# Two transformer blocks on one core: 1024 instead of 512 bytes a partition for the descriptors of GpSimd's DMAs, and a table of constants without one unread block

## The chip, the cores and the metric

One core of one Trainium2 chip runs the kernel. A time is that of one execution on the device in microseconds (us), and a kernel's time is the median over its runs. Before the change it is 4043.69 us, from two runs of 4041.86 and 4045.51 us.

## The reference

Two model blocks run one after the other over 512 tokens of width 1024, each with two layers, all in fp32. The parts that take most of the time are the SwiGLU stages and the other projections. There are six SwiGLU stages: two in each layer of the first block (width 2816) and one in each layer of the second (`FFN_HIDDEN`, the same).

```python
def swiglu(h, w_gate, w_up, w_down):
    return (jax.nn.silu(h @ w_gate) * (h @ w_up)) @ w_down

def first_block(...):
    for l in range(DEPTH):
        x = x + 0.5 * swiglu(rms_norm(x, ffn1_norm[l]), ffn1_w_gate[l], ffn1_w_up[l], ffn1_w_down[l])
        h = rms_norm(x, mix_norm[l])
        ...
        x = x + jnp.concatenate([y_a, y_b, y_c], axis=-1) @ w_out[l]
        x = x + memory_cross_attention(rms_norm(x, xa_norm[l]), rms_norm(mem, mem_norm[l]),
                                       xa_wq[l], xa_wkv[l], xa_wo[l])
        x = x + 0.5 * swiglu(rms_norm(x, ffn2_norm[l]), ffn2_w_gate[l], ffn2_w_up[l], ffn2_w_down[l])
    return rms_norm(x, final_norm)

def second_block(...):
    for l in range(DEPTH):
        ...
        h = h + mix @ w_out[l]
        u = rmsnorm(h, ffn_norm[l])
        h = h + (jax.nn.silu(u @ w_gate[l]) * (u @ w_up[l])) @ w_down[l]
    return rmsnorm(h, final_norm)
```

The conv, sparse attention, cross attention, retention and differential attention between them are left out here; the change does not touch them.

## The kernel before

Activations stay in SBUF, transposed, with 128 features on the partitions. Every weight comes in chunks of 128 output columns by 1024 inputs (512 KB, 4 KB a partition). A product is made in three matmuls of rounded fp32 parts: high weight by high input, high by low, low by high. So each chunk has to be split into `w_hi` and `w_lo`. There are four slots (`RING = 4`) for the raw chunk, for `w_hi` and for `w_lo`; chunk n uses slot n % 4.

A chunk passes through these steps, each ordered by semaphores alone:

- SP loads it from HBM into `raw` (`load`, L457), when the low part of the chunk that had the slot before is finished (`wait_split`).
- ACT rounds it into `w_hi` (L1102), when PE has finished the chunk that had the slot before (`tiles`).
- The low part is made in one of two ways. In the mixing and attention stages DVE subtracts (L1562). For the chunks of the list `LOW`, 68 from the fifth chunk of each SwiGLU stage on, ACT writes a second, negated rounding into `w_lo` (L1104), and GpSimd (POOL) issues a DMA from `raw` to `w_lo` that adds in flight (`low`, L2272). The DMA's completion counts up `low_in` of its slot.
- PE waits for the low part (`wait_split`) and multiplies: 8 x 3 matmuls of 128 x 512 (L563, L564, L565).

```python
def low(c):
    pool.wait_ge(rounded, c + RING + 1)
    nc.gpsimd.dma_start(w_lo[:, c % RING, :], raw[:, c % RING, :], accum_op=ALU.add).then_inc(low_in[c % RING], 16)
```

The argument c is that of the chunk before in the slot: `low(c)` finishes chunk c + 4. POOL's code has no wait on `low_in`. 404 chunks go this way.

A SwiGLU stage has 68 chunks in three groups: 8, 8 and 6 tiles of the width, each as turns of four chunks (gate, up, gate, up), 11 turns in all, and 8 down chunks behind each group (six instead of eight blocks deep in the last). In nearly all turns the last two chunks are a fast pair: `fast_pair` makes the 256-column halves with seven products of half size instead of eight (84 matmuls of 128 x 256, L604, L605, L606), for which it needs sums of the weights' quarters. POOL makes these sums from `raw` (`first_sums`, L2288 and L2289, which wait for the loads of both chunks, and `second_sums`, L2294 and L2295); ACT rounds them (`sum_hi`, L1148), DVE makes the rest. In a turn POOL's order is written out by hand:

```python
low(c)
if ahead: first_sums(*pairs[0])
low(c + 1)
if ahead: second_sums(*pairs.pop(0))
low(c + 2)
low(c + 3)
```

Between the down chunks of a stage's last group POOL also squares x for the next norm (L2245, L2246), and DVE adds a finished down chunk to x (L1652).

Constants come in one table, `constants()`, loaded at the start by two DMAs on SP: columns 0 to 255 first (identity and ones), the rest later. Columns are named by `C_ID` and its companions (L60); `C_ROT` is written into the table and read by nothing.
Of the kernel before, what the change touches and what calls it, by code (L numbers as in the profile page):

```python
# [32 lines left out]
P = 128  # L33
# [23 lines left out]
ROUND = 1.5 * 2 ** 23  # L57

C_ID, C_ONE, C_ROT, C_DIST, C_NEG, C_DEC, C_BIG, C_INV = 0, 128, 256, 384, 896, 1408, 1920, 2048  # L60
C_N = C_INV + 1

# [90 lines left out]
def constants():  # L154
    c = np.zeros((P, C_N), np.float32)
    p = np.arange(P)[:, None]
    m = np.arange(S)[None, :]
    c[:, C_ID:C_ID + P] = np.eye(P)
    for j in range(P):
        c[j + 32 if j % 64 < 32 else j - 32, C_ROT + j] = 1.0  # L160
    dist = 384 + p - m
    c[:, C_DIST:C_DIST + S] = dist
    c[:, C_NEG:C_NEG + S] = np.where(dist >= 0, 0.0, -BIG)
    c[:, C_DEC:C_DEC + S] = np.where(m - p >= 0, m - p, 1e9)
    c[:, C_BIG:C_BIG + P] = np.where(np.arange(P)[None, :] <= p, 0.0, BIG)
    inv = (10000.0 ** (-np.arange(0, 64, 2) / 64)).astype(np.float32)
    c[:, C_INV] = inv[np.arange(P) % 32] * np.where(np.arange(P) % 64 < 32, 1.0, -1.0)
    c[:, C_ONE:C_ONE + P] = 1.0
    return c
# [2282 lines left out]
```

## Time and profile before

| what | value |
|---|---|
| median of 2 runs | 4043.69 us |
| profiled execution, its own time | 4040.94 us |
| its span, first to last instruction | 4039.1 us |
| PE busy, share of the span | 89% |
| granted clock of PE, mean | 0.965 |
| POOL busy, share of the span | 30% |
| low DMAs (`w_lo<-raw`) | 404 of 512 KB |
| raw loads | 602 |

The profile is of one execution. PE is TensorE's matmuls, DVE VectorE, ACT ScalarE, POOL GpSimd and SP SyncE, whose queue issues the loads. A line number such as L2272 is that of the kernel before. Waits are put down to whatever released the engine last; "issue" stands where the profile shows no releaser. [...]

### The profile page before, as it was taken

To read this page: it belongs to the slowest core of one execution; us is meant where nothing else is said; L and a number is where in the kernel's file an instruction comes from. 1 tells how busy PE (TensorE), PEld (TensorE's weight loads), DVE (VectorE), ACT (ScalarE), POOL (GpSimd) and SP (SyncE) were. 2 spreads that over 40 slices of the span, in tenths; PEclk is the share of its full clock that TensorE was granted. 3 is DMA by queue.
4 is the path that set the end of the run, shared out by engine and by line. 5 is a ranking of instruction groups with operands and counts; after the bars stand their busy time and mean duration, and the time that the engine had idled before them with its cause. 6 is when DMAs were issued, how large, how long until landed. Compare 5 with 4: busy or idle time off the path is not lost.

```text
span 4039.1 us, 50532 instructions
## 1 busy us (share of the span) xinstructions
PE 3596.7 (89%) x18454; PEld 2928.2 (72%) x18454; DVE 1912.6 (47%) x2971; ACT 1791.8 (44%) x2567; POOL 1229.0 (30%) x1035
## 2 busy tenths in 40 slices
PE   8888899998888888879999988889988888998887
PEld 6677686877767677757687776777877667886766
DVE  4333497564324524349756532445644244572423
ACT  5444356345434444435634543434544343453433
POOL 1223375132223422236513232330423131042323
PEclk9999899999999999999999999999999999999999
DMA  7676641426766666664242666642366663246665
GB/s 179 159 163 157 146 110 58 122 79 148 162 156 153 159 157 158 155 150 108 61 118 82 149 157 156 152 119 63 94 156 157 155 154 101 59 113 151 159 150 129
DMA packets 679460, 536.52 MB, mean 133 GB/s; under 512 B 19952, under 2 KB 622984, under 8 KB 679304
## 3 DMA queue, kind: packets, MB, share of 16 engines
q1 hardware_dynamic: 617096, 317.15, 27.7%
q0 software_dynamic: 58176, 211.84, 26.7%
q10 hardware_dynamic: 4032, 5.51, 0.6%
q8 instruction: 91, 1.49, 0.2%
q14 instruction: 65, 0.53, 0.0%
HBM read 314.75 MB, written 2.10 MB: 78 GB/s over the span
## 4 chain that ended last, share of the span: by engine, by line
PE 39%; DMA 24%; issue 18%; POOL 11%; ACT 5%; DVE 3%; ACTq 0%; POOLq 0%; SPq 0%; DVEq 0%
DMA w_lo<-raw 17%; PE bank L563 10%; PE bank L565 10%; PE bank L564 10%; DMA raw<-in_ffn_w_up 2%; ACT w_lo L1104 2%; POOL mem L2246 2%; POOL w_lo L2272 2%; POOL mem L2245 2%; POOL mem L2289 1%; ACT w_hi L1102 1%; PE bank L718 1%; POOL mem L2295 1%; DMA raw<-in_w_up 1%; POOL mem L2294 1%
## 5 line engine op out<-in xcount | busy, mean ns | idle before, releaser
L1102 ACT ACTIVATE w_hi<-raw 128x1024 fp32r<-128x1024 f32 x602 | 635.2, 1058 | 1509.4 <-PE bank L565 1366.6
L563 PE MATMUL bank<-u_hi,w_hi 128*128 128x512 f32 x1920 | 793.8, 413 | 156.6 <-DMA w_lo<-raw 144.0
L2272 POOL DMA_DIRECT2D w_lo<-raw x404 | 356.4, 882 | 1679.3 <-issue 1100.3
L563 PE MATMUL bank<-h_hi,w_hi 128*128 128x512 f32 (+1 forms) x1568 | 636.9, 406 | 174.8 <-DMA w_lo<-raw 162.5
L565 PE MATMUL bank<-u_hi,w_lo 128*128 128x512 f32 x1920 | 779.9, 406 | 0.0
L564 PE MATMUL bank<-u_lo,w_hi 128*128 128x512 f32 x1920 | 777.0, 405 | 0.0
L565 PE MATMUL bank<-h_hi,w_lo 128*128 128x512 f32 (+1 forms) x1568 | 619.9, 395 | 0.0
L564 PE MATMUL bank<-h_lo,w_hi 128*128 128x512 f32 (+1 forms) x1568 | 619.5, 395 | 0.0
L563 PEld LDWEIGHTS bank<-u_hi,w_hi 128*128 128x128 f32 x1920 | 373.7, 195 | 278.2 <-issue 120.7
L563 PEld LDWEIGHTS bank<-h_hi,w_hi 128*128 128x128 f32 x1568 | 303.8, 194 | 290.3 <-issue 156.8
L1652 DVE SCALAR_TENSOR_TENSOR x<-bank,x 128x512 f32 (+1 forms) x192 | 132.6, 690 | 741.4 <-PE bank L565 741.4
L565 PEld LDWEIGHTS bank<-u_hi,w_lo 128*128 128x128 f32 x1920 | 372.6, 194 | 91.4
L564 PEld LDWEIGHTS bank<-u_lo,w_hi 128*128 128x128 f32 x1920 | 374.1, 195 | 86.0
L1104 ACT ACTIVATE w_lo<-raw 128x1024 fp32r<-128x1024 f32 x404 | 421.4, 1043 | 0.0
L565 PEld LDWEIGHTS bank<-h_hi,w_lo 128*128 128x128 f32 x1568 | 303.8, 194 | 69.1
L1562 DVE TENSOR_TENSOR w_lo<-raw,w_hi 128x1024 fp32r<-128x1024 f32 x198 | 280.9, 1425 | 150.7 <-ACT w_hi L1102 150.6
L564 PEld LDWEIGHTS bank<-h_lo,w_hi 128*128 128x128 f32 x1568 | 304.3, 194 | 62.9 <-issue 0.5
L2382 POOL TENSOR_TENSOR mem<-mem,spare 128x512 f32<-128x512 f32 x120 | 171.1, 1464 | 113.2 <-ACT spare L1327 112.9
L604 PE MATMUL bank<-t_hi,sum_hi 128*128 128x256 f32 x684 | 190.0, 278 | 0.0
L605 PE MATMUL bank<-t_lo,sum_hi 128*128 128x256 f32 x684 | 189.6, 277 | 0.0
L606 PE MATMUL bank<-t_hi,sum_lo 128*128 128x256 f32 x684 | 189.4, 277 | 0.0
L1566 DVE SCALAR_TENSOR_TENSOR u_lo<-x,par,u_hi (+1 forms) x88 | 140.8, 1600 | 79.4 <-ACT u_hi L1109 79.4
(302 smaller groups left out, 5969.5 us busy)
## 6 DMA issues: line engine op xcount, KB each, us to landing
w_lo<-raw POOLq DMA_DIRECT2D x404, 512.0 KB, 6.2
raw<-in_w_in SPq DMA_DIRECT2D x96, 512.0 KB, 3.9
raw<-in_ffn_w_gate SPq DMA_DIRECT2D x88, 512.0 KB, 4.0
raw<-in_ffn_w_up SPq DMA_DIRECT2D x88, 512.0 KB, 4.0
raw<-in_ffn_w_down SPq DMA_DIRECT2D x64, 512.0 KB, 4.2
raw<-in_w_gate SPq DMA_DIRECT2D x44, 512.0 KB, 3.9
raw<-in_w_up SPq DMA_DIRECT2D x44, 512.0 KB, 3.9
raw<-in_w_out SPq DMA_DIRECT2D x32, 512.0 KB, 4.1
```

What stands on the lines that cost most here:

```text
L563: mm(o, w_hi[:, s, w], rhs_hi[:, r], start=k == order[0], stop=False)
L564: mm(o, w_hi[:, s, w], rhs_lo[:, r], start=False, stop=False)
L565: ins = mm(o, w_lo[:, s, w], rhs_hi[:, r], start=False, stop=k == order[-1])
L604: mm(o, wh, rh, start=k == 0, stop=False)
L605: mm(o, wh, rl, start=False, stop=False)
L606: ins = mm(o, wl, rh, start=False, stop=k == KT // 2 - 1)
L1102: ins = a(w_hi[:, p.slot, :], raw[:, p.slot, :], ACT.Copy)
L1104: ins = a(w_lo[:, p.slot, :], raw[:, p.slot, :], ACT.Copy, scale=-1.0)
L1562: tt(w_lo[:, p.slot, :], raw[:, p.slot, :], f32(w_hi[:, p.slot, :]), ALU.subtract).then_inc(split, 1)
L1566: stt(dst_lo, src, scale, f32(dst_hi), ALU.mult, ALU.subtract).then_inc(e, 1)
L2272: nc.gpsimd.dma_start(w_lo[:, c % RING, :], raw[:, c % RING, :], accum_op=ALU.add).then_inc(low_in[c % RING], 16)
L2382: tt(conv[n % 2], conv[n % 2], tap_t[n % 4], ALU.add).then_inc(tap_added, 1)
```

## The change

The scratch for the descriptors of POOL's DMAs grows from 512 to 1024 bytes in each partition. The block `C_ROT`, 128 columns of fp32 or 512 bytes in each partition, leaves the table, and the columns behind it move up by 128; `C_N` falls from 2049 to 1921. On SP the DMA of the table's rest moves 1665 columns instead of 1793. No other instruction differs on any engine, and the order on each is as before. The tensors in front of `const` lie 512 bytes further on, those behind it where they were.

```diff
-C_ID, C_ONE, C_ROT, C_DIST, C_NEG, C_DEC, C_BIG, C_INV = 0, 128, 256, 384, 896, 1408, 1920, 2048
+C_ID, C_ONE, C_DIST, C_NEG, C_DEC, C_BIG, C_INV = 0, 128, 256, 768, 1280, 1792, 1920
 C_N = C_INV + 1
...
     c[:, C_ID:C_ID + P] = np.eye(P)
-    for j in range(P):
-        c[j + 32 if j % 64 < 32 else j - 32, C_ROT + j] = 1.0
     dist = 384 + p - m
...
-    nc = bacc.Bacc("TRN2", target_bir_lowering=False, num_devices=1, dynamic_dma_scratch_size=512)
+    nc = bacc.Bacc("TRN2", target_bir_lowering=False, num_devices=1, dynamic_dma_scratch_size=1024)
```

## Rows read from the trace of the kernel before

**Rows 1.** The page: span, busy time of each engine, and the chain that ended last, by engine.

```profile
span 4039.1 us, 50532 instructions
...
PE 3596.7 (89%) x18454; PEld 2928.2 (72%) x18454; DVE 1912.6 (47%) x2971; ACT 1791.8 (44%) x2567; POOL 1229.0 (30%) x1035
...
PE 39%; DMA 24%; issue 18%; POOL 11%; ACT 5%; DVE 3%; ACTq 0%; POOLq 0%; SPq 0%; DVEq 0%
```

**Rows 2.** Stretches: us, PE, PEld, DVE, ACT, POOL busy (count), clock, DMA share, GB/s.

```profile
34.00:480.00 446.00, 381.88 (x1803) 306.42 (x1802) 159.35 (x224) 196.06 (x219) 122.14 (x116) 0.95 0.69 158
...
3610.00:4024.00 414.00, 350.93 (x1846) 290.24 (x1844) 149.75 (x205) 175.17 (x192) 121.13 (x112) 0.97 0.65 149
sum 2575.00, PE 2197.17 PEld 1804.80 DVE 978.38 ACT 1132.46 POOL 762.64; mean PE 366.19 PEld 300.80 DVE 163.06 ACT 188.74 POOL 127.11
...
1800.00:2210.00 410.00, 399.75 (x2053) 316.54 (x2053) 292.26 (x524) 196.56 (x363) 159.86 (x112) 0.99 0.33 92
```

**Rows 3.** Waits: engine, line, waited for: us in total, times, longest.

```profile
POOL w_lo L2272 <- issue: 1100.3, 235, 7.2
...
POOL w_lo L2272 <- ACT w_lo L1104: 559.6, 110, 7.0
...
PE bank L563 <- DMA w_lo<-raw: 306.5, 195, 4.9
...
PE bank L604 <- DMA w_lo<-raw: 20.1, 30, 1.6
```

**Rows 4.** SP in order of time: start us, us, queue, line, op, out<-in.

```profile
1620.94 0.38 SPq L457 DMA_DIRECT2D raw<-in_ffn_w_gate  x1
1627.35 0.38 SPq L457 DMA_DIRECT2D raw<-in_ffn_w_up  x1
1633.87 0.37 SPq L457 DMA_DIRECT2D raw<-in_ffn_w_gate  x1
...
1647.14 0.37 SPq L457 DMA_DIRECT2D raw<-in_ffn_w_gate  x1
```

**Rows 5.** POOL in order of time, same stretch; idle before and its releaser in brackets.

```profile
1621.24 0.86 POOL L2272 DMA_DIRECT2D w_lo<-raw  x1 [6.86 <-ACT w_lo L1104]
1627.64 0.89 POOL L2272 DMA_DIRECT2D w_lo<-raw  x1 [5.54 <-issue]
1634.12 0.87 POOL L2272 DMA_DIRECT2D w_lo<-raw  x1 [5.59 <-issue]
```

**Rows 6.** The tile w_lo: ACT's second rounding, ns min/median/max, and its DMAs' landing.

```profile
L1104 ACT ACTIVATE w_lo<-raw x404: 1038/1043/1055, 33.5 to 4000.9; 128x1024 fp32r<-128x1024 f32 x135
...
DMA to landing us min/median/max: 4.5/6.2/8.0
```

**Rows 7.** DVE in order of time: a chunk of the down projection taken.

```profile
297.21 0.69 DVE L1652 SCALAR_TENSOR_TENSOR x<-bank,x 128x512 f32 x1 [4.91 <-PE bank L565]
```

**Rows 8.** The page: DMA queues, packets, MB, their packets' time as share of the span.

```profile
q1 hardware_dynamic: 617096, 317.15, 27.7%
q0 software_dynamic: 58176, 211.84, 26.7%
```

**Rows 9.** PE in order of time: matmul starts and modelled durations at either clock.

```profile
1623.58 0.63 PE L563 MATMUL bank<-h_hi,w_hi 128*128 128x512 f32 x1
1624.00 0.63 PE L564 MATMUL bank<-h_lo,w_hi 128*128 128x512 f32 x1
...
1624.80 0.40 PE L563 MATMUL bank<-h_hi,w_hi 128*128 128x512 f32 x1
1625.03 0.40 PE L564 MATMUL bank<-h_lo,w_hi 128*128 128x512 f32 x1
```

**Rows 10.** The chain in order of time: a load, the first and the last sum.

```profile
1640.74 3.88 DMA raw<-in_ffn_w_up
...
1644.79 1.28 POOL mem L2288
...
1648.76 1.31 POOL mem L2295
```

## The prediction

> **What bounds the kernel now.** I read the page's first parts, then stretches, then who waits for whom, then two engines side by side around the longest wait. TensorE (PE) is busy 89% of the span, but the chain that ended last gives PE only 39%; 24% of it is DMA and 18% "issue", time in which an engine waited for nothing that the profile shows [rows 1]. So something between DMAs sets part of the time. The stretches say where: in the six SwiGLU stages, together 2575 us of the 4039.1 us span, PE is busy 2197.17 us, 85%, at a granted clock of 0.95 to 0.97; in the stretch 1800:2210, between two such stages, it is busy 399.75 of 410 us at 0.99 [rows 2]. The waits name the late operand: 195 + 30 waits of PE, 306.5 + 20.1 us, end when a DMA `w_lo<-raw` lands. POOL (GpSimd), which issues these DMAs (I call them low DMAs), stood 1100.3 us, 235 times, in front of them for no reason that the profile names [rows 3].
>
> The reason can be read from two engines. SP's load into a raw slot waits, in the code, for the landing of the low DMA that read this slot. SP starts its loads at 1620.94, 1627.35 and 1633.87 [rows 4]. POOL starts its next low DMA at 1621.24, 1627.64 and 1634.12 [rows 5], 0.25 to 0.30 us later each time, although its code waits only for ACT's rounding (to which the first of the three is put down, and 559.6 us in all [rows 3]). So POOL acts as if it too waited for the landing: one low DMA is in flight, never two. From issue to landing one takes 6.2 us at the median [rows 6]; with the gap that is the period of 6.4 to 6.5 us in rows 5. PE needs less: in the down projection DVE takes a finished chunk every 4.91 + 0.69 = 5.60 us where PE does not wait [rows 7]. A serial DMA sets the pace of these stages. 
>
> [...]
>
> **The change part by part: the scratch.** No instruction is added, removed or moved on any engine. The sum is made against the profiled execution's 4040.94 us (span 4039.1), 2.75 us below the median of 4043.69. If a second low DMA fits, POOL issues as soon as ACT has rounded, and three costs go. First, PE's waits that end with a landing, 306.5 + 20.1 = 326.6 us [rows 3]. Second, PE's idle time is counted from the modelled end of a matmul, 0.40 us after its start, while matmuls that don't wait start 0.23 us apart [rows 9]; so each of the 225 waits costs 0.17 us more than is shown, 38 us. Third, the clock: a mean of 0.96 means that 8% of 2575 us, 206 us, ran at 1.2 GHz. There matmuls start 0.42 us apart instead of 0.23 [rows 9], so 45% of the busy part (85%) is lost: 206 x 0.85 x 0.45 = 79 us. I expect it back, since the clock is 0.99 where PE hardly waits [rows 2]. Together 444 us.
>
> A second way gives the same. A turn of four chunks is two plain ones and a fast pair, 48 matmuls of 512 columns and 84 of 256; at 0.233 us (5.60 / 24) and half of it 21.0 us. A down chunk is 5.6 us, or 4.2 in the last group of a stage. Eleven turns, 16 and 8 chunks are 354 us a stage and 2125 for six: 450 below the 2575 of rows 2, which also hold waits of other kinds. So 444 is a ceiling.
>
> **What is late next.** The DMA engines first. The two queues' packets took 26.7% and 27.7% of the span [rows 8], which is 2.67 us for a low DMA (404) and 1.86 us for a load (602): 4.5 us a chunk, under PE's 5.3 to 5.6; in the last groups (six of eight chunks, where loads are three quarters) 4.1 against 4.2. I charge 0.4 us to each of those 48 chunks, 20 us. Next, the slots: a slot is free when PE is done with its chunk and is wanted again three chunks later, after some 16 us. ACT's two roundings of 1.04 us and a landing of 6.2, at most 8.0 [rows 6], are 8.3 to 10.1, so some 6 us are left for queueing. Last, POOL's own order: the sums of weights wait for a load (3.88 us in the chain) and take 1.3 us each, four a turn [rows 10]; the next low DMA is queued behind them on POOL, and ACT's `sum_hi` waits for the last. A landing 6.2, a load 3.9, four sums 5.2 and three low DMAs of 0.9 on POOL make 18 us of a turn of 21; with longer landings it reaches 21. I charge 25 us for this over the stages. That leaves 444 - 45 = 399 us. The ends are nothing and 444.
>
> **The dropped block.** 128 columns are 64 KB less to load at the start, 0.3 us at a low DMA's 512 KB in 2.67 us, beside the other loads there: 0 taken. x, raw, w_hi and w_lo lie 512 bytes further into a partition; no instruction's wait or shape hangs on the address, and nothing in the rows sets one slot apart from another: 0 taken.
>
> The sum: 4040.94 - 399 = 3642, and 3 more for the median: 3645 us.
>
> **The rivals.** *It isn't the scratch.* POOL may take these DMAs one at a time whatever room they have, because they accumulate, or because two don't fit in 1024 bytes either. [...] Against it: nothing in the code orders them, and room is what a DMA on POOL's queue needs besides. The time stays at 4041 to 4044 us. Chance 7%.
>
> *Lifted, but paid to the DMA engines.* Low DMAs and loads now run into each other. The engines are busy 0.65 to 0.69 of these stages [rows 2]; the same work in 2125 us would be 0.67 x 2575 / 2125 = 0.81. If landings stretch so that half of the waits stay, 444 / 2 = 222 us go, about 3820 us. Against it stand the 6 us of room. Chance 12%.
>
> *Slower: loads starved behind low DMAs.* Today a load starts at a landing, ahead of the next low DMA. With several low DMAs queued it would come among their packets. A slot then goes through landing, load, ACT 2.1, low DMA 6.2, and four chunks take 26.2 us today (1620.94 to 1647.14 [rows 4]); when loads take over 26.2 - 8.3 = 17.9 us, against 3.9 now, the kernel becomes slower. If each of a load's 64 packets per engine (617096 packets for some 602 loads on 16 engines) waits for one packet of a low DMA, 2.67 / 8 = 0.33 us, that is 21 + 1.9 us, a turn of 31.2, and over 101 turns 5.0 x 101 = 505 us more: about 4550 us. Against it: the four low DMAs of a turn hold the engines for 10.7 us in all, so a load can hardly wait for 21. Chance 3%. [...]
>
> **How the numbers follow.** My forecast, most of the waits gone, has 78%; its own range is 3560, some 40 us under the ceiling's 3597 since the rows round, to 3780, 260 us gone. The contention case at 3820 lies just above and is still more than 2% faster. The range 3560 to 3780 leaves 2 in 10 outside. Two per cent, 81 us, is about what a measurement of this kernel can tell from no change. Faster by over 2%: 78 + 12 = 90%; within 2%: 7%; slower: 3%.
>
> **What would show it.** Right: "issue" in front of POOL's low DMAs falls from 1100 us to little, and what ends POOL's idle time there is ACT's rounding; low DMAs start less than a landing apart; PE's waits on `w_lo<-raw` fall from 327 to under 60 us; the clock in the six stages rises to 0.98 or more; down chunks come 5.6 us apart throughout; the DMA share there passes 0.75. Landings may grow to 7 or 8 us without harm. Wrong: POOL still starts 0.3 us behind SP at each landing (first rival); or low DMAs overlap, but PE waits for their landing, or ACT and POOL for raw loads, as long as before (second and third).

## The result, and the profile after

The changed kernel takes 3543.71 us (median of two runs, 3534.69 and 3552.73) against 4043.69 before: a ratio of 0.8764, 95% interval 0.8666 to 0.8861. It is 500 us faster, 100 us more than forecast, and lies below the range of 3560 to 3780. The direction and the cause hold; the size was off. Every line number is two less than before, as two lines are gone (L2272 is L2270, L563 is L561).

The page after, with the lines that answer to [rows 1] and [rows 8]:

```profile
span 3531.6 us, 50532 instructions
...
PE 3447.1 (98%) x18454; PEld 2869.0 (81%) x18454; DVE 1984.7 (56%) x2971; ACT 1780.2 (50%) x2567; POOL 1221.3 (35%) x1035
...
q0 software_dynamic: 58176, 211.84, 33.9%
q1 hardware_dynamic: 617096, 317.08, 31.0%
...
PE 66%; DMA 10%; POOL 8%; DVE 6%; issue 5%; ACT 3%; ACTq 0%; POOLq 0%; DVEq 0%; SPq 0%
```

PE is now busy 98% and has 66% of the chain; DMA and "issue" fell from 42% together to 15%. The same packets are moved in a shorter span. The stretches that hold the same matmuls as those of [rows 2], to within two each: the first and the last of six, and their sum (columns as there). Behind them stands the stretch between two stages, which holds some more matmuls than the one there:

```profile
34.00:394.00 360.00, 352.92 (x1802) 295.18 (x1801) 175.55 (x216) 194.08 (x219) 121.84 (x116) 1.00 0.88 194
...
3174.00:3519.00 345.00, 334.51 (x1848) 286.48 (x1847) 161.45 (x204) 173.01 (x191) 120.82 (x112) 0.99 0.81 178
sum 2104.00, PE 2062.51 PEld 1757.46 DVE 1053.61 ACT 1115.42 POOL 768.45; mean PE 343.75 PEld 292.91 DVE 175.60 ACT 185.90 POOL 128.08
```

```profile
1545.00:1968.00 423.00, 412.69 (x2123) 327.90 (x2122) 305.36 (x543) 202.58 (x371) 170.68 (x119) 0.99 0.34 95
```

The six stages took 2575 us and take 2104; PE is busy 98% of them instead of 85%, at a clock of 0.99 to 1.00 instead of 0.95 to 0.97, with the DMA engines at 0.81 to 0.90 instead of 0.65 to 0.69. Between the stages nothing moved: PE is busy 98% there at 0.99, before and after. The waits, as in [rows 3]:

```profile
POOL w_lo L2270 <- ACT w_lo L1102: 984.8, 261, 6.7
...
POOL mem L2286 <- DMA raw<-in_ffn_w_up: 214.8, 35, 9.4
...
POOL mem L2286 <- DMA raw<-in_w_up: 120.2, 18, 9.4
...
PE bank L561 <- DMA w_lo<-raw: 20.5, 16, 1.8
...
PE bank L573 <- POOL mem L2244: 0.7, 4, 0.2
```

"Issue" in front of POOL's low DMAs is gone from the list; what ends POOL's idle time is ACT's rounding. PE's waits on a landing fell from 326.6 to 20.5 us. A piece of POOL's and DVE's time in the down projection, to compare with [rows 5] and [rows 7]:

```profile
255.88 0.88 POOL L2270 DMA_DIRECT2D w_lo<-raw  x1 [4.73 <-ACT w_lo L1102]
261.48 0.87 POOL L2270 DMA_DIRECT2D w_lo<-raw  x1 [4.72 <-ACT w_lo L1102]
```

```profile
253.63 0.69 DVE L1650 SCALAR_TENSOR_TENSOR x<-bank,x 128x512 f32 x1 [4.91 <-PE bank L563]
259.24 0.69 DVE L1650 SCALAR_TENSOR_TENSOR x<-bank,x 128x512 f32 x1 [4.91 <-PE bank L563]
264.83 0.69 DVE L1650 SCALAR_TENSOR_TENSOR x<-bank,x 128x512 f32 x1 [4.91 <-PE bank L563]
```

Both go at PE's pace now, 5.60 us, no longer at a DMA's 6.4 to 6.5. The landings, first of the low DMAs, then of all that touches `raw` (the loads and the low DMAs):

```profile
DMA to landing us min/median/max: 4.5/5.9/9.7
```

```profile
DMA to landing us min/median/max: 3.1/5.6/11.7
```

The first was 4.5/6.2/8.0. The 512 KB loads of the SwiGLU stages land after 5.5 to 6.5 us at the median (`in_w_gate` alone after 4.0), where they took 3.9 to 4.4. So loads do land later with several low DMAs in flight, and it costs PE little: 20.5 us of waits on a landing are left.

How many low DMAs are in flight follows from the issues and landings in the traces (of 404 issues, how many were the first, second or third in flight):

```
kernel                 first  second  third   what an issue waited for
before (512 bytes)       404       0      0   333 times 0.31 us after the landing before
after (1024)              99     259     46   no landing of an earlier one
```

### The profile page after: what moved, and what is told of

Read it like the earlier page. It is cut to its first block, busy times and chain, and to the rows that moved or that the text cites. A ratio compares the mean times of both kernels' runs of the same rounds, so it can differ in the third digit from the quotient of the medians.

```text
span 3531.6 us, 50532 instructions
## 1 busy us (share of the span) xinstructions
PE 3447.1 (98%) x18454; PEld 2869.0 (81%) x18454; DVE 1984.7 (56%) x2971; ACT 1780.2 (50%) x2567; POOL 1221.3 (35%) x1035
## 3 DMA queue, kind: packets, MB, share of 16 engines
q0 software_dynamic: 58176, 211.84, 33.9%
## 4 chain that ended last, share of the span: by engine, by line
PE 66%; DMA 10%; POOL 8%; DVE 6%; issue 5%; ACT 3%; ACTq 0%; POOLq 0%; DVEq 0%; SPq 0%
PE bank L561 16%; PE bank L563 16%; PE bank L562 16%; DMA w_lo<-raw 5%; PE bank L602 3%; PE bank L604 3%; PE bank L603 3%; POOL mem L2244 2%; DMA raw<-in_ffn_w_up 2%; POOL mem L2243 2%; PE bank L716 1%; POOL w_lo L2270 1%; DMA raw<-in_w_up 1%; PE bank L717 1%; PE bank L718 1%
## 5 line engine op out<-in xcount | busy, mean ns | idle before, releaser
L561 PE MATMUL bank<-u_hi,w_hi 128*128 128x512 f32 x1920 | 765.5, 399 | 22.9 <-DMA w_lo<-raw 20.5
L563 PE MATMUL bank<-u_hi,w_lo 128*128 128x512 f32 x1920 | 762.9, 397 | 0.0
L562 PE MATMUL bank<-u_lo,w_hi 128*128 128x512 f32 x1920 | 758.3, 395 | 0.0
L2270 POOL DMA_DIRECT2D w_lo<-raw x404 | 354.3, 901 | 1002.6 <-ACT w_lo L1102 984.8
L561 PE MATMUL bank<-h_hi,w_hi 128*128 128x512 f32 (+1 forms) x1568 | 610.2, 389 | 19.1 <-DVE h_lo L1564 18.4
L563 PE MATMUL bank<-h_hi,w_lo 128*128 128x512 f32 (+1 forms) x1568 | 607.4, 387 | 0.0
L562 PE MATMUL bank<-h_lo,w_hi 128*128 128x512 f32 (+1 forms) x1568 | 604.9, 386 | 0.0
L561 PEld LDWEIGHTS bank<-u_hi,w_hi 128*128 128x128 f32 x1920 | 361.2, 188 | 120.3 <-issue 32.7
L563 PEld LDWEIGHTS bank<-u_hi,w_lo 128*128 128x128 f32 x1920 | 361.3, 188 | 86.5
L562 PEld LDWEIGHTS bank<-u_lo,w_hi 128*128 128x128 f32 x1920 | 361.4, 188 | 84.9
L561 PEld LDWEIGHTS bank<-h_hi,w_hi 128*128 128x128 f32 x1568 | 295.2, 188 | 89.5 <-DVE h_lo L1564 23.6
L563 PEld LDWEIGHTS bank<-h_hi,w_lo 128*128 128x128 f32 x1568 | 295.2, 188 | 65.8
L2286 POOL TENSOR_TENSOR mem<-raw 128x512 f32<-128x512 f32 x57 | 80.8, 1418 | 338.8 <-DMA raw<-in_ffn_w_up 214.8
L1564 DVE SCALAR_TENSOR_TENSOR u_lo<-x,par,u_hi (+1 forms) x88 | 156.5, 1778 | 64.4 <-ACT u_hi L1107 64.4
L602 PE MATMUL bank<-t_hi,sum_hi 128*128 128x256 f32 x684 | 189.9, 278 | 0.0
```

Of the source, the lines that this page charges most:

```text
L561: mm(o, w_hi[:, s, w], rhs_hi[:, r], start=k == order[0], stop=False)
L562: mm(o, w_hi[:, s, w], rhs_lo[:, r], start=False, stop=False)
L563: ins = mm(o, w_lo[:, s, w], rhs_hi[:, r], start=False, stop=k == order[-1])
L602: mm(o, wh, rh, start=k == 0, stop=False)
L1564: stt(dst_lo, src, scale, f32(dst_hi), ALU.mult, ALU.subtract).then_inc(e, 1)
```

## The experiments

All times stand beside runs of the kernel before on the same chip, 4030 to 4031 us in both sets. The kernel after had stood beside 4043.69 us, so the experiments are set against it by ratio; its own, 0.8764, is known to about 1%.

**e1. One part alone: the block dropped, the scratch as before.**

```diff
 # kernel after
-dynamic_dma_scratch_size=1024
+dynamic_dma_scratch_size=512
```

> The kernel after with the scratch back at 512 bytes; the block of constants stays dropped. Theory (room for descriptors): 4035 to 4050 us, within 0.3% of before; POOL's low DMAs start 0.3 us after the landing of the one before, 'issue' in front of them near 1100 us. Rival (the dropped block or the shifted addresses bring part of the gain): below 4000 us.

Measured: 4030.02 us, ratio 0.9994 (0.9985 to 1.0004). The row in front of POOL's low DMAs is that of before:

```profile
POOL w_lo L2270 <- issue: 1124.2, 243, 6.7
```

The dropped block is worth nothing. In e1, x, raw, `w_hi` and `w_lo` lie where they lay before; that their shift by 512 bytes is worth nothing either follows from e2 and e7 below, which differ in the scratch, and so in this shift, alone and take 3947.8 and 3945.32 us. So the whole gain is the room in the scratch.

**e2. The serial order put back by hand, at 1024 bytes.**

```diff
 def low(c):
     pool.wait_ge(rounded, c + RING + 1)
+    if c + RING - 1 in LOW:
+        pool.wait_ge(low_in[(c - 1) % RING], low_count(c + RING - 1) * 16)
     nc.gpsimd.dma_start(...)
```

> The kernel after (1024 bytes) with one wait added: POOL waits, before each low DMA, for the landing of the low DMA before it. Theory (one low DMA in flight is the whole cause): 4000 to 4050 us, PE's waits on w_lo<-raw back at 300 to 340 us, PE's wait on POOL's squares back at 35 to 45 us, the clock back at 0.965. Rival (the larger scratch helps in another way too, such as faster descriptor writing): clearly below 4000 us, at 3700 to 3900.

Measured: 3947.8 us, ratio 0.9791 (0.9775 to 0.9808). One DMA in flight brings most of the loss back, with the waits:

```profile
PE bank L561 <- DMA w_lo<-raw: 237.6, 198, 4.0
PE bank L573 <- POOL mem L2244: 40.8, 4, 10.3
...
PE bank L602 <- DMA w_lo<-raw: 15.9, 29, 1.3
```

The wait on POOL's squares is back whole, the waits on a landing only to 253.5 us, not to 300 or more. The kernel is 2.1% faster than before and lies between the ranges of the theory and of the rival, though its POOL starts later after a landing. That is taken up with e7 below.

**e3 and e4. The same wait in two parts: only in the last down group of each stage, where POOL squares x between its low DMAs; and only everywhere else.**

```diff
 # kernel of e2_serial_all
+    # e3: c in LAST_DOWN; e4: c not in LAST_DOWN
+    # LAST_DOWN = [c for n in FFN_AT for c in range(n + N_FFN - KT, n + N_FFN)]
-    if c + RING - 1 in LOW:
+    if c + RING - 1 in LOW and c in LAST_DOWN:
```

> The kernel after with that wait only in front of the low DMAs that POOL issues between the squares, in the last down group of each of the six stages (44 of 404). Theory (what is queued behind the waiting low DMA on POOL costs too): PE's wait on POOL's squares comes back with 35 to 45 us over four or five stage ends, with waits on landings and the clock some 100 to 160 us more than after: 3640 to 3710 us. Rival (only waits that end with a landing count): 44 DMAs are 11% of 404, so 11% of 444 us, 50 us: 3590 us, and no wait of PE on POOL's squares.

> The kernel after with that wait in front of all other low DMAs (360 of 404). Theory: the two parts add up to the whole of some 500 us, so 340 to 400 us more than after: 3880 to 3950 us, with no wait of PE on POOL's squares above 5 us. Rival: 89% of 444 us is 395 and the rest of the gain is in the clock everywhere, so 3980 to 4010 us.

Measured: 3618.42 us, ratio 0.8988 (0.8965 to 0.9012), and 3857.59 us, 0.9562 (0.9546 to 0.9578). PE's waits of e3, then of e4 (both kernels have two lines more than after ahead of these, so the line numbers are those of before):

```profile
PE bank L575 <- POOL mem L2246: 41.2, 4, 10.6
...
PE bank L563 <- DMA w_lo<-raw: 26.8, 22, 1.9
```

```profile
PE bank L563 <- DMA w_lo<-raw: 193.7, 169, 4.3
...
PE bank L604 <- DMA w_lo<-raw: 17.0, 31, 1.4
...
PE bank L575 <- POOL mem L2246: 0.5, 3, 0.2
```

The two waits come apart cleanly. In e3, PE's wait on landings is only 6.3 us longer than after, and the wait on POOL's squares is all back: 41.2 us. So the rival, by which only waits that end with a landing count, is out. e3's profiled span is 75 us longer than that of after: 40.5 us of this are the squares' wait, 6.3 us landings, 12.8 us waits of PE that the profile names "issue", and 12.3 us a longer busy time of PE, at a mean clock of 0.986 instead of 0.994. My 3640 to 3710 was too high, since I had also expected landing waits there.

In e4 the squares' wait is absent. Its time lies below the 3880 to 3950 that I expected, and its rival's 3980 to 4010 is further off. The losses against after, 2.2% (e3) and 8.0% (e4) of before, add up to that of e2, 10.3%; I had expected them to add up to the loss of before, 12.4%.

**e5. Where the next low DMA fits: 576 bytes.**

```diff
-dynamic_dma_scratch_size=1024
+dynamic_dma_scratch_size=576
```

> [...]

Measured: 3527.51 us, ratio 0.8755 (0.8737 to 0.8773), as fast as after. With two low DMAs in flight I had expected 3540 to 3580 us, so it is 12 us below that; with one in flight (the rival) 4020 to 4050 us, and with three (the second rival) the time of after. How many 576 bytes hold was my estimate; no run had shown it. 316 issues were second in flight, none third, and 87 of them came 0.31 us after the landing of the one two before, none sooner: two fit, exactly. One in flight and three are out. Two don't fit in 512 bytes, two do in 576, and three in 1024. If the room is simply shared out among the DMAs in flight, one low DMA takes more than 512 / 2 = 256 and at most 576 / 2 = 288 bytes of each partition, an estimate from these sizes. What fills this room, no trace shows.

**e8. Two in flight by hand, at 1024 bytes** (the wait of e2 with c - 2 and RING - 2 in place of c - 1 and RING - 1).

> The kernel after (1024 bytes) with POOL waiting in its code for the landing of the low DMA two before, so that at most two are in flight. Theory (two are enough, as PE is then the bound): within 1% of after, 3530 to 3570 us. Rival (the third matters): 3580 us or more, with PE's waits on w_lo<-raw above 60 us.

Measured: 3529.27 us, ratio 0.8754 (0.8739 to 0.8769), with PE's waits on landings as after:

```profile
PE bank L561 <- DMA w_lo<-raw: 22.7, 20, 2.1
```

Room for a third is worth nothing; the step from one to two is everything.

**e6. The order on POOL, at 512 bytes: squares ahead of the low DMA.**

```diff
 # kernel before, squares_and_low, for each k
-low(n + k)
 ...
 pool.wait_ge(taken, n + k + RING + 1)
 ...
 add_square(k)
+low(n + k)
```

> The kernel before (512 bytes) with one change of order: in a stage's last down group POOL squares a chunk ahead of the low DMA of that turn, not behind it, so that a low DMA that waits for the one before delays no square. Theory (work queued behind the low DMA on POOL costs): PE's wait on POOL's squares falls from 42 to under 5 us, and with the clock the time falls by 40 to 70 us: 3960 to 3995 us. Rival (the low DMAs, issued later by a square, delay the next stage's chunks as much): 4020 to 4045 us.

Measured: 4007.14 us, ratio 0.9946 (0.9930 to 0.9963). That is 23 us gained where I expected 40 to 70: more than the noise, but between the two ranges. The wait itself speaks for the theory:

```profile
PE bank L575 <- POOL mem L2246: 16.5, 4, 5.3
```

The wait went from 41.8 to 16.5 us, its longest from 11.2 to 5.3, not to the 5 us expected, and the waits on landings did not grow, as the rival has it (313.7 us, from 326.6). The last square has left its low DMA behind, but still stands behind the one of the turn before (462.94), which waited for a landing:

```profile
462.94 0.88 POOL L2272 DMA_DIRECT2D w_lo<-raw  x1 [2.83 <-issue]
463.55 1.35 POOL L2245 TENSOR_TENSOR mem<-x 128x512 f32<-128x512 f32 x1
464.98 2.17 POOL L2246 TENSOR_TENSOR mem<-mem 128x512 f32<-128x512 f32 x1
469.54 0.90 POOL L2272 DMA_DIRECT2D w_lo<-raw  x1 [2.39 <-issue]
```

**e7. The way of waiting: e2's wait at 512 bytes.** The ring, here and below, is the scratch for the descriptors of POOL's DMAs, not the kernel's four slots (`RING`).

```diff
 # kernel of e2_serial_all
-dynamic_dma_scratch_size=1024
+dynamic_dma_scratch_size=512
```

> The kernel of e2_serial_all (POOL waits for the landing before in its own code) with the scratch back at 512 bytes. e2 was 80 us faster than before with one low DMA in flight in both; its landings came 0.3 us sooner. If the way of waiting makes that difference (the ring's own wait against a semaphore wait in POOL's code): 3940 to 3960 us, period 6.26 us. If the size of the ring does: 4020 to 4035 us, period 6.5 us.

Measured: 3945.32 us, ratio 0.9788 (0.9771 to 0.9804). It is not the size of the ring; the way of waiting alone is worth 2.1%. The low DMAs' landings of e1 (the ring's own wait, 512 bytes) and of e7 (a semaphore wait in POOL's code, 512 bytes):

```profile
DMA to landing us min/median/max: 4.5/6.1/7.2
```

```profile
DMA to landing us min/median/max: 4.5/5.5/7.5
```

## Why the prediction was right and wrong

**What bounds: right.** One low DMA in flight, held by the ring's room, set the pace. That 512 bytes hold one and 1024 more than one was a premise of the forecast, which no row of before shows. The table of issues shows one in flight before; e5 shows that 64 bytes more of scratch lift it and bring the whole gain; e1, with e2 and e7, shows that nothing else in the change matters; and e2 and e7 show that one in flight costs most of the gain by itself.

**The signs named in advance.** Those of being right came: "issue" gone; low DMAs overlapping; the stages' clock at 0.99 to 1.00; chunks 5.60 us apart; the DMA share above 0.75; PE's landing waits under 60 us. One named as a sign of being wrong came too: POOL waits longer, not shorter, for the raw loads before its sums, 214.8 + 120.2 us after. Before, it was:

```profile
POOL mem L2288 <- DMA raw<-in_ffn_w_up: 106.6, 35, 4.8
POOL mem L2288 <- DMA raw<-in_w_up: 53.8, 18, 3.5
```

It did not reach PE, whose list of waits after has no row for the products that use the sums (L602 to L604). The rivals are out: 305 of 404 low DMAs are issued with another in flight, and the time lies far below 3820 us.

**The size: the step that failed is "Together 444 us ... So 444 is a ceiling".** It was built on the waits of PE that end with a landing, and took them, with the clock and the overlap of matmuls, for all that a serial DMA costs. PE's time splits as follows, from the two profiles (span less busy, and busy).

| | before | after | less |
|---|---|---|---|
| PE idle | 442.4 | 84.5 | 357.9 |
| of it on a landing | 326.6 | 20.5 | 306.1 |
| of it on POOL's squares | 41.8 | 0.7 | 41.1 |
| of it named "issue" | 16.9 | 1.6 | 15.3 |
| PE busy | 3596.7 | 3447.1 | 149.6 |

- *Left out: what was queued behind the waiting instruction on its own engine.* I weighed POOL's queue only for what would be late next, in the sums, and not for what was late already. The row was there before, second in the list of PE's waits, and I did not read it:

```profile
PE bank L575 <- POOL mem L2246: 41.8, 4, 11.2
```

  It is the norm's statistic at four stage ends. The order on POOL at the first of them, before:

```profile
463.68 0.89 POOL L2272 DMA_DIRECT2D w_lo<-raw  x1 [2.95 <-issue]
464.29 1.35 POOL L2245 TENSOR_TENSOR mem<-x 128x512 f32<-128x512 f32 x1
465.72 2.13 POOL L2246 TENSOR_TENSOR mem<-mem 128x512 f32<-128x512 f32 x1
470.21 0.90 POOL L2272 DMA_DIRECT2D w_lo<-raw  x1 [2.35 <-issue]
470.82 1.36 POOL L2245 TENSOR_TENSOR mem<-x 128x512 f32<-128x512 f32 x1
472.26 1.26 POOL L2246 TENSOR_TENSOR mem<-mem 128x512 f32<-128x512 f32 x1
```

  The last square starts at 470.82, behind a low DMA that the ring holds back until 470.21, 0.32 us after the landing before. PE does not need that DMA yet: it goes on at 475.30, before the DMA lands at 476.42. PE takes the statistic when the square is done:

```profile
473.58 1.86 PE L575 MATMUL bank<-ones_r,mem 128*128 128x1 f32 x8 [9.35 <-POOL mem L2246]
...
475.88 0.63 PE L564 MATMUL bank<-u_lo,w_hi 128*128 128x512 f32 x1
476.30 0.63 PE L565 MATMUL bank<-u_hi,w_lo 128*128 128x512 f32 x1
```

  The matmuls behind it start 0.42 us apart: the granted clock was 0.5 from 467.60 to 481.25, so they ran slow too. After the change the low DMAs at this place wait only 0.4 to 0.6 us, for ACT's rounding, and the granted clock stays at 1.00:

```profile
386.80 0.90 POOL L2270 DMA_DIRECT2D w_lo<-raw  x1 [0.63 <-ACT w_lo L1102]
387.41 1.37 POOL L2243 TENSOR_TENSOR mem<-x 128x512 f32<-128x512 f32 x1
```

  The statistic waits 0.2 us at most. e3 brings this wait back, 41.2 us, in a span 75 us longer; by the ratios it is 2.2% of before, 90 us, with the 1% of doubt in after's.
- *Mis-sized: the clock and the matmuls' overlap.* I had 79 + 38 = 117 us; PE's busy time fell by 149.6. The 1.2 GHz in the first term stands in no run: the traces give the granted clock as a share of full speed, either 1.00 or 0.50, and before, from 461 to 463 us, at 1.00, matmuls of 128x512 start 0.23 us apart, from 476 to 481 us, at 0.50, 0.42 to 0.43 us. I counted the clock in the six stretches only. Over the whole span the mean went from 0.965 to 0.994, that is half-speed time from 283 to 42 us; at the loss that I used (0.85 x 0.45) it is 92 us instead of 79. The other 58 us, where I had 38 for the overlap, were not separated.
- *Mis-sized: the charge for what comes late next.* 45 us were charged, 20.5 us of landing waits are left. The longer waits of POOL for loads, shown above, did not become waits of PE.

Together 41 + 33 + 25 us, and the 15 us of waits named "issue", which I had not counted, are 114 us. These last go with the serial order in the last groups, too (14.4 us in e3, 4.9 in e4); what they wait for, no run shows. PE's remaining waits grew by 5, which leaves 109: the spans differ by 507.5 us, 108.5 more than 399.

**Why the second way agreed with a wrong ceiling.** It set 68 chunks a stage, 1980 matmuls by its own count, against stretches that hold 1800 to 1939: the very matmuls of those 2575 us take 2104 after, with all their remaining waits, where I had 2125 without any. That it came out at 450 beside 444 was chance.

**Another split, by kind of edit.** Of the 12.4% gained, the ring's own way of waiting is 2.1% (e7), the serial order in the last groups 2.2% (e3 against after) and elsewhere 8.0% (e4 against after); the sum is 12.3%. The two parts against after share the 1% of doubt in its ratio.

## What to carry to other kernels

A transfer that is issued one at a time charges more than the waits that end with its landing: everything behind it in the issuing engine's program is late as well, and those waits stand in the list under another name. So read all of PE's waits, go back from each releaser along its own engine, and ask what held it. When GpSimd's DMAs start a fixed short time after the landing before (0.31 us here), look at the scratch for descriptors: room for a second DMA in flight was worth 12% here, for a third nothing.

## What was not expected of the hardware

The ring's own wait costs more than time to wait. With one low DMA in flight in every case, POOL's own semaphore wait started the next DMA some 0.6 us after a landing (e2 and e7) instead of 0.31 (before, e1), and yet the next landing came sooner, so that the median period was 6.26 and 6.20 us instead of 6.53 and 6.49. In the packets, the raw load that runs ahead of the low DMA is nearly done (95% of its packets) 3.0 to 3.1 us after the landing before, instead of 3.3 to 3.4 before and in e1, though SP issued it as early. The low DMA's own first packet comes after 2.82 us in e2 and e7, and after 2.99 before and 2.91 in e1; so it is not that a low DMA which starts later leaves the load alone for longer. Nor is it the size of the ring (e7 has 512 bytes). What the ring's wait does to a load on another queue stays open; it was not tried further.

By the three sizes of the scratch (512 bytes: no issue second in flight; 576: 316 second, none third; 1024: 46 third), an accumulating DMA over 128 partitions took more than 256 and at most 288 bytes of each partition, the estimate made at e5. The trace shows 9 packets per engine and DMA (58176 for 404 DMAs on 16 engines), 8 of 4096 bytes and one of 4; what is kept in the scratch, it does not show.
